# First attention layer of a fused two-block kernel: index projections first, selection dealt out in rounds, attention in head pairs, output projection in two halves

## The chip, the cores and the metric

The kernel runs on one core of a Trainium2 chip. The metric is device time in microseconds (us) of one execution. A core has TensorE (matrix products into PSUM), VectorE, ScalarE, GpSimd (POOL in the rows) and SyncE (SP, which issues DMAs). Each engine works through its own list of instructions in order, and the engines meet only at semaphores, which the kernel raises and waits for by hand.

## The reference, cut to what matters

Two blocks run one after the other on 512 tokens of width 1024. The second block prepends 16 meta tokens (528 positions) and has two attention layers. The change is in the first of these, a sparse attention that picks 128 keys for each query:

```python
q, k, v, qi, ki, wi = jnp.split(h @ w_in, A_SPLITS, axis=-1)      # 1024, 256, 256, 512, 64, 8 columns
q = rms_norm(q.reshape(B, Tp, N_HEADS, A_HEAD_DIM), gq)           # 8 heads of 128
k = rms_norm(k.reshape(B, Tp, A_KV_HEADS, A_HEAD_DIM), gk)        # 2 key/value heads
# for each block of queries
s = jnp.einsum('bqhd,bsd->bqhs', qib, ki) * IDX_DIM ** -0.5       # 8 index heads of 64
score = jnp.einsum('bqh,bqhs->bqs', wib, jax.nn.relu(s))
score = jnp.where(vis[None], score, NEG_INF)
_, idx = lax.top_k(score, k_top)                                  # 128 keys
# bias by relative position, softmax over the chosen keys, values
logits = jnp.einsum('bqgrd,bqkgd->bqgrk', qg, ksel) * scale + bias
o = jnp.einsum('bqgrk,bqkgd->bqgrd', softmax(logits), vsel)
out = o.reshape(...) @ w_o ;  h = h + out
```

## The kernel before, in words

**Numbers and weights.** Activations lie transposed, features on partitions and 528 positions along the row. A projection is computed to fp32 accuracy from two parts: weight and activation are each split into `hi` and `lo`, and TensorE does hi x hi, hi x lo and lo x hi. One output tile of 128 features takes 8 x 3 x 2 = 48 matmuls of 264 columns (L480). Its weights come by a DMA of 512 KB on SP's queue into `w_raw`, ScalarE makes `w_hi` (L405), VectorE makes `w_lo` (L411). Two slots of each let the splits of tile g+2 follow the products of tile g. The small fp32 matmuls (index scores, logits, transposes, values) are two records each in the profile.

**Queries in blocks.** The 528 queries are one block of 16 (i = 0) and four of 128 (i = 1 to 4). Block i sees 16, 144, 272, 400 or 528 keys. The selection finds the 128 largest scores of each query row by 16 rounds of MAX8 (the eight largest) and MATCH_REPLACE8 (strike them out), L2121 and L2122. From what was struck out comes a mask (`selm`, L2127), which GpSimd adds to the bias of each head (`msb`, L1030).

**The old order of this layer.** First all 17 tiles of `w_in_a` (`pa`, `kw`): q, k, v, index queries, and one with the index key and the head weights. ScalarE evacuates (L1245), GpSimd multiplies by the norm's inverse root (L612), and between tiles the ten q and k tiles are normalised by head: square, sum by TensorE (L1645), root, an inverse over 128x528 (L2089), product (L2090). Then 40 combinations (block i, head h), i outermost, in `combosA`. For each: logits on TensorE (L746, L748), bias and row maximum on VectorE (L2136), exponential on ScalarE (L1297), inverse and scaling on VectorE (L2153, L2154), transposes (L755, L757), their copies (L1310, L1313), the values' product (L766) and its copy (L1319). Logits of a combination, values of the one two before and transposes of the one before follow each other on TensorE. Ahead of the first head of a block i > 0 stand its eight index scores, the weighted sum of their relu on VectorE (L2111, L2115), the 16 rounds and the mask. At the end o is split, and the output projection `oa` has 8 tiles of 48 matmuls, which VectorE adds to the residual.

The second attention layer (another kind, `qkv` in the code) is already written with its projection tiles between the steps of the attention and with two heads to a step. The change doesn't touch its order; its lines (L1729 tiles, L1765 logits, L1784 and L1787 transposes, L1801 and L1803 values, L1385 exponentials, L2251 and L2254 row maxima, L1744 sums of squares by head) serve as a comparison.

## Time and profile before

| what | us |
|---|---|
| median of 3 runs | 2784.76 (2784.76 to 2785.87) |
| profiled execution, its own time | 2784.07 |
| its span | 2782.0 |
| TensorE busy | 2511.2 (90%) |
| VectorE busy | 1427.3 (51%) |
| ScalarE busy | 1038.6 (37%) |
| GpSimd busy | 489.1 (18%) |
| granted TensorE clock, mean | 0.922 |

The page divides the span into 40 slices of 69.6 us. In slices 20 to 23 (counted from 1), 1321 to 1600 us, where this attention layer lies, TensorE's digits are 6, 7, 5 and 7 against 8 and 9 nearly everywhere else, and those of the granted clock 6, 5, 5 and 8. A clock of 1.00 means 2.4 GHz and 0.50 means 1.2 GHz. How to read it: a stage in which TensorE has no gaps is bound by TensorE. Where it has gaps, the view of waits says which engine it waited for, and the chain of waits in order of time shows the pieces in which TensorE had no part.

### The profile page before, as it was taken

How to read it: one execution, taken by the hardware profiler on the slowest of the kernel's cores; microseconds unless marked ns; L12 is line 12 of the kernel's file. 1: busy time of each engine (PE TensorE's matmuls, PEld its weight loads, DVE VectorE, ACT ScalarE, POOL GpSimd, SP SyncE). 2: the span in 40 equal slices, each digit the busy share in tenths (PEclk: the TensorE clock that was granted, in tenths of full speed). 3: DMA queues.
4: the chain of work that ended last, by engine and by line, in shares of the span. 5: the costliest groups of instructions: out<-in, count | busy, mean ns of one | idle time of the engine just before them, and what ended most of it. 6: DMA issues, size and time to landing. Idle time of an engine off the chain costs nothing.

```text
span 2782.0 us, 41428 instructions
## 1 busy us (share of the span) xinstructions
PE 2511.2 (90%) x15393; PEld 2206.8 (79%) x15393; DVE 1427.3 (51%) x2067; ACT 1038.6 (37%) x1792; POOL 489.1 (18%) x427
## 2 busy tenths in 40 slices
PE   5898888999879999969675799999989989999998
PEld 4677766788658878859543699999988867999998
DVE  6895455522444324255756556664334344666631
ACT  5543444432523223223332333332245543333322
POOL 0000224431360000352101121110000000211100
PEclk8998999999989989979655899999999977999999
DMA  7561111332322333323100023333332210333322
GB/s 262 166 181 31 38 32 41 90 96 81 93 69 85 96 110 95 98 77 84 37 1 0 16 84 90 90 90 91 91 111 62 70 47 27 87 90 90 89 88 89
DMA packets 386952, 227.17 MB, mean 82 GB/s; under 512 B 10562, under 2 KB 377893, under 8 KB 386853
## 3 DMA queue, kind: packets, MB, share of 16 engines
q1 hardware_dynamic: 378085, 191.14, 24.3%
q0 software_dynamic: 8160, 32.53, 3.2%
q10 hardware_dynamic: 608, 2.16, 0.2%
q8 instruction: 65, 1.06, 0.2%
q14 instruction: 34, 0.28, 0.0%
HBM read 220.82 MB, written 4.85 MB: 81 GB/s over the span
## 4 chain that ended last, share of the span: by engine, by line
PE 76%; DVE 9%; issue 7%; ACT 3%; DMA 2%; POOL 2%; SPq 0%; POOLq 0%; ACTq 0%; DVEq 0%
PE PS L480 60%; PE PS L1729 5%; DMA w_raw<-in_w_in_dram 1%; DVE ada_acc L626 1%; PE PS L766 1%; PE PS L1586 1%; PE PS L1765 1%; PE PS L1801 1%; ACT w_hi L405 1%; DVE w_lo L411 1%; PE PS L1803 1%; PE PS L1598 1%; DVE conv_acc L1929 1%; DMA w_ada<-in_w_ada_dram 1%; POOL square L707 1%
## 5 line engine op out<-in xcount | busy, mean ns | idle before, releaser
L411 DVE TENSOR_TENSOR w_lo<-w_raw,w_hi 128x1024 fp32r<-128x1024 f32 x360 | 482.8, 1341 | 759.4 <-ACT w_hi L405 759.1
L480 PE MATMUL PS<-op_hi,w_hi 128*128 128x264 f32 (+3 forms) x2536 | 696.4, 329 | 45.3 <-DVE op_lo L582 16.2
L480 PE MATMUL PS<-op_lo,w_hi 128*128 128x264 f32 (+3 forms) x2536 | 690.1, 326 | 0.0
L480 PE MATMUL PS<-op_hi,w_lo 128*128 128x264 f32 (+3 forms) x2536 | 687.1, 325 | 0.0
L480 PEld LDWEIGHTS PS<-op_hi,w_hi 128*128 128x128 f32 (+2 forms) x2536 | 428.0, 190 | 102.8 <-issue 23.0
L405 ACT ACTIVATE w_hi<-w_raw 128x1024 fp32r<-128x1024 f32 x360 | 379.0, 1053 | 221.5 <-PE PS L480 200.3
L480 PEld LDWEIGHTS PS<-op_hi,w_lo 128*128 128x128 f32 (+2 forms) x2536 | 426.7, 191 | 38.3 <-issue 0.7
L480 PEld LDWEIGHTS PS<-op_lo,w_hi 128*128 128x128 f32 (+2 forms) x2536 | 427.1, 191 | 36.7 <-issue 0.9
L480 PE MATMUL PS<-ff_hi,w_hi 128*128 128x264 f32 (+1 forms) x960 | 242.2, 312 | 0.0
L480 PE MATMUL PS<-ff_hi,w_lo 128*128 128x264 f32 (+1 forms) x960 | 242.2, 312 | 0.0
L480 PE MATMUL PS<-ff_lo,w_hi 128*128 128x264 f32 (+1 forms) x960 | 242.1, 312 | 0.0
L1336 ACT ACTIVATE ff_u<-PS 128x528 f32<-128x528 f32 x88 | 53.9, 613 | 336.8 <-PE PS L480 317.3
L612 POOL TENSOR_TENSOR ff_u<-ff_u,rstd 128x528 f32<-128x528 f32 x88 | 100.3, 1141 | 421.7 <-ACT ff_u L1336 392.7
L480 PEld LDWEIGHTS PS<-ff_lo,w_hi 128*128 128x128 f32 x960 | 157.0, 188 | 9.9
L480 PEld LDWEIGHTS PS<-ff_hi,w_hi 128*128 128x128 f32 x960 | 156.9, 188 | 9.9
L480 PEld LDWEIGHTS PS<-ff_hi,w_lo 128*128 128x128 f32 x960 | 156.7, 188 | 10.0
L766 PE MATMUL PS<-probsT,v_tokA 128*128 128x128 f32 (+2 forms) x240 | 60.1, 387 | 76.1 <-ACT probsT L1313 75.6
L766 PEld LDWEIGHTS PS<-probsT,v_tokA 128*128 128x128 f32 (+1 forms) x240 | 45.2, 257 | 103.1 <-ACT probsT L1313 93.7
L679 POOL TENSOR_TENSOR sumsq<-sumsq,evac 128x528 f32<-128x528 f32 x21 | 28.0, 1332 | 515.9 <-ACT evac L662 515.9
L2065 DVE TENSOR_TENSOR norm_v<-evac 128x512 f32<-128x512 f32 x32 | 22.2, 692 | 107.2 <-ACT evac L1224 107.2
L2192 DVE SCALAR_TENSOR_TENSOR ff_c<-ff_u,param_cols,ff_c 128x528 f32<-128x528 f32 x88 | 69.8, 793 | 12.6 <-DVE ff_c L2191 6.7
L2191 DVE SCALAR_TENSOR_TENSOR ff_c<-ff_u,param_cols,ff_c 128x528 f32<-128x528 f32 x88 | 67.7, 769 | 12.6 <-DVE ff_c L2189 6.7
(403 smaller groups left out, 3743.5 us busy)
## 6 DMA issues: line engine op xcount, KB each, us to landing
w_raw<-in_w_up_dram SPq DMA_DIRECT2D x120, 512.0 KB, 3.8
w_raw<-in_w_in_dram SPq DMA_DIRECT2D x64, 512.0 KB, 4.1
w_raw<-in_w_down_dram SPq DMA_DIRECT2D x64, 512.0 KB, 3.7
w_ada<-in_w_ada_dram POOLq DMA_DIRECT2D x12, 2048.0 KB, 10.2
...
```

Of the source, the lines that this page charges most:

```text
L405: act.activation(whi[slot][:], wraw[slot][:], ACT.Copy).then_inc(sem("w_hi_ready"), 1)
L411: dve.tensor_tensor(wlo[slot][:], wraw[slot][:], whi[slot][:].bitcast(F32), ALU.subtract).then_inc(sem("w_split"), 1)
L480: last = pe.matmul(a[0:l.cols, h, 0:cn], w[slot][:, k, 0:l.cols], x[:, kk, c0:c0 + cn], start=(j == 0 and k == 0 and w is whi and x is l.h ...
L612: pool.tensor_tensor(x, x, rs[0:L[name].cols, :], ALU.mult).then_inc(sem("scaled"), 1)
L626: ins = dve.scalar_tensor_tensor(acc[:], w[:, k, :], small[:, 8 + k:9 + k], acc[:], ALU.mult, ALU.add)
L679: pool.tensor_tensor(sacc[:, :], sacc[:, :], et[g % 2][:, :], ALU.add).then_inc(sem("sumsq_ready"), 1)
L707: squared = link.mark(pool.tensor_tensor(sqt[:, c0:T], e, e, ALU.mult))
L766: last = pe.matmul(PS[:, b, 0:nq], v(t)[0:rows, :], p[0:rows, t, 0:nq], start=(t == 0), stop=(t == ntile - 1))
L1336: act.activation(halves(uu[par][:, 2:2 + T]), acc_view(l, par), ACT.Copy).then_inc(sem("evacuated"), 1)
L1729: last = pe.matmul(PS[:, h, 0:TH], w[slot][:, k, :], x[:, k, h * TH:(h + 1) * TH], start=(k == 0 and w is whi and x is hi), stop=(k == KD ...
L2191: link(dve.scalar_tensor_tensor(c[:, :], u[:, 1:1 + T], w(1), c[:, :], ALU.mult, ALU.add))
L2192: dve.scalar_tensor_tensor(c[:, :], u[:, 0:T], w(0), c[:, :], ALU.mult, ALU.add).then_inc(sem("ff_conv"), 1)
```

## The change

1. **Order of the tiles** (`TILES_A`): the four index-query tiles, the tile with index key and head weights, then k0, q0 to q3, v0, k1, q4, q5, v1, q6, q7. The first five run alone. The other twelve stand in slots 0 to 11 of a list of 22 slots, one tile each.
2. **Selection.** Index scores and their sums of block s+1 stand in slot s (0 to 3). The 64 rounds are dealt out over slots 0 to 12 (`ROUNDS`, rounds before and after the index sum). There are four relu buffers for two, and scores and masks of all four blocks have places of their own.
3. **Steps.** 16 steps (`STEPS_A`), each a pair of heads d and a batch b of query blocks (b = 0 is blocks 0 and 1, then one block each), run from slot 5 to 20. A slot has the logits of step n, a tile, the values of step n-1 and the transposes of step n. The values' product is now laid out by queries, so the division by the row sum is done in its copy (`outA`), and o is turned back by transposes (`turn_headA`) in slots 15, 16, 20, 21 and after.
4. **Norms.** Nothing is multiplied by the norm's inverse root over whole tiles. q and k are normalised from sums of squares by head, gathered by small matmuls in a 32x132 tile, in four batches (slots 3, 5, 9, 12). That tile takes a root and an inverse, goes to DRAM and comes back spread over all partitions (`head_rows_A`, on SP's queue). v takes its factor in its copy.
5. **Output projection.** `oa1` with o of heads 0 to 3, 8 half tiles of 24 matmuls, five in slots 17 to 21 and three after; `oa2` with heads 4 to 7, 8 half tiles. Both are added to the residual.

The core of the diff:

```diff
+        TILES_A = ("i0", "i1", "i2", "i3", "kw", "k0", "q0", "q1", "q2", "q3", "v0", "k1", "q4", "q5", "v1", "q6", "q7")
-        L["pa"] = Linear(plan, 16, wsrc(I["w_in_a_2"][0], 0), HH, HL, block1=False)
-        L["kw"] = Linear(plan, 1, wsrc(I["w_in_a_2"][0], 2048), HH, HL, cols=72, block1=False)
-        L["oa"] = Linear(plan, KD, wsrc(I["w_o_a_2"][0], 0), OAh, OAl, block1=False)
+        L["ia"] = Linear(plan, 17, lambda g, t, par, j, kt, cols: ia_src(g), HH, HL, block1=False)
+        for half in range(2):
+            L[f"oa{half + 1}"] = Linear(plan, KD, down_src(I["w_o_a_2"][0], 4 * half), *((HH, HL), (OAh, OAl))[half],
+                                        kts=(4,), block1=False)
+        SLOTS_A = 22
+        STEPS_A = [(0, 0), (0, 1), (1, 0), (1, 1), (0, 2), (1, 2), (2, 0), (2, 1), (0, 3), (1, 3), (3, 0), (2, 2), (3, 1),
+                   (2, 3), (3, 2), (3, 3)]
+        NORM_SLOT = {3: 0, 5: 1, 9: 2, 12: 3}
+        ROUNDS = {0: (0, 5), 1: (10, 0), 2: (6, 0), 3: (4, 0), 4: (3, 0), 5: (5, 0), 6: (5, 0), 7: (5, 0), 8: (5, 0),
+                  9: (4, 0), 10: (3, 0), 11: (5, 0), 12: (4, 0)}
+        FIRST_PART = 17
...
             # SyncE
+            def head_rows_A(b):
+                sp.wait_ge(sem("hn_rec"), b + 1)
+                sp.dma_start(head_scratch[b], head_msA[:]).then_inc(sem("hn_rows"), 16)
+                sp.wait_ge(sem("hn_rows"), 16 * (b + 1))
+                for n, (_, sq) in enumerate(NORM_TILES[b]):
+                    src = bass.AP(head_scratch.tensor, b * 32 * 132 + n * 132, [[0, P], [8 * 132, 4], [1, 132]])
+                    sp.dma_start(sq[:, :].rearrange("p (q n) -> p q n", q=4), src).then_inc(sem("hn_bc"), 16)
...
             # TensorE
+            def logitsA(n):
+                d, b = STEPS_A[n]
...
+                if n:
+                    pe.wait_ge(sem("A_max"), n)
+                    pe.wait_ge(sem("A_pt"), 2 * n)
...
+            for s in range(SLOTS_A):
+                n = step_at(s)
+                if s in NORM_SLOT:
+                    head_squaresA(s)
+                if s in (6, 10):
+                    turn_valuesA(s)
+                if s in (15, 16, 20, 21):
+                    turn_headA({15: 0, 16: 2, 20: 4, 21: 5}[s])
+                if n is not None:
+                    logitsA(n)
+                if s < 12:
+                    projectA(5 + s)
+                if s >= FIRST_PART:
+                    partA(s - FIRST_PART)
...
+                if s < 4:
+                    index_scores(s + 1)
...
+                if 0 <= s - 6 < len(STEPS_A):
+                    headsA(s - 6, s)
+                if n is not None:
+                    turn_probsA(n)
+                if s in (15, 16):
+                    turn_headA({15: 1, 16: 3}[s])
...
             # ScalarE
+                if n is not None:
+                    expA(n)
+                if s < 12:
+                    project_outA(5 + s)
...
+                if s < 4:
+                    index_relu(s + 1)
+                if 0 <= s - 6 < len(STEPS_A):
+                    outA(s - 6)
+                if n is not None:
+                    probs_outA(n)
...
             # VectorE
+                if n is not None:
...
+                    row_maxesA(n)
+                if norm is not None:
+                    dve.wait_ge(sem("hn_std"), norm + 1)
+                    dve.reciprocal(head_msA[:], head_msA[:]).then_inc(sem("hn_rec"), 1)
+                if s:
+                    select(ROUNDS.get(s, (0, 0))[0])
+                if s - 1 in NORM_SLOT:
+                    head_scaleA(NORM_SLOT[s - 1])
+                if s < 12:
+                    split_nextA(L["ia"], 5 + s)
+                if s < 4:
...
+                    index_sum(s + 1)
+                    select(ROUNDS[s][1])
+                if n is not None:
+                    sums_inverse(n)
```

VectorE before, at the end of the selection for query block 1; the lines are those of the code before (L2121 and L2122 one round, L2127 the mask, L2136 bias and row maximum of head 0, whose number behind a name is a buffer):

```order
L2121 MAX top_142<-idx_work 128x8
L2122 MATCH_REPLACE idx_work<-top_142,idx_work 128x144
L2127 TENSOR_SCALAR sel_mask<-idx_work 128x144
L2136 ISA probs_136,maxes<-PS,bias_sel_130 128x144
L2136 ISA maxes 128x1
L2143 TENSOR_SCALAR maxes<-maxes 128x1
L2153 RECIPROCAL maxes<-maxes 128x1
```

VectorE now, from the end of slot 7 into slot 8 (lines of the changed code: L422 weight split, L2387 inverse of the row sums, L2370 row maxima of two heads at 272 keys, L2347 and L2348 a round at 400 keys):

```order
L422 TENSOR_TENSOR w_lo_57<-w_raw_53,w_hi_55 128x1024
L2387 RECIPROCAL statsA<-statsA 128x4
L2370 ISA probsA_145,statsA<-PS,bias_sel_136 128x272
L2370 ISA statsA 128x1
L2370 ISA probsA_146,statsA<-PS,bias_sel_137 128x272
L2370 ISA statsA 128x1
L2378 TENSOR_SCALAR statsA<-statsA 128x2
L2347 MAX statsA<-idx_work 128x8
L2348 MATCH_REPLACE idx_work<-statsA,idx_work 128x400
```

Rounds of one block now stand behind the row maxima of steps with fewer keys, with a weight split between them.

TensorE before, in query block 4 (L757 and L755 transposes of one head, L748 the logits of the next, L766 the values of the one before):

```order
L757 MATMUL PS<-mats,probs_136 128x128 x4
L748 MATMUL PS<-projA 128x264 x2
L766 MATMUL PS<-probsT_141,v_tokA 128x128 x5
L755 MATMUL PS<-mats,probs_134 16x128
L757 MATMUL PS<-mats,probs_134 128x128 x4
```

TensorE now, from the end of the tile of slot 7 (L1752) into slot 8: values of a step (L1867, L1869), transposes of the next (L1847, L1850), then the logits of slot 8 (L1831) and the first products of its tile:

```order
L1752 MATMUL PS<-op_hi,w_lo_57 128x264 x2
L1867 MATMUL PS<-v_tokA,probsTA_147 128x128 x2
L1869 MATMUL PS<-v_tokA,probsTA_147 128x128
L1867 MATMUL PS<-v_tokA,probsTA_148 128x128 x2
L1869 MATMUL PS<-v_tokA,probsTA_148 128x128
L1850 MATMUL PS<-mats,probsA_143 16x16
L1847 MATMUL PS<-mats,probsA_143 128x128
L1850 MATMUL PS<-mats,probsA_143 16x128
L1850 MATMUL PS<-mats,probsA_144 16x16
L1847 MATMUL PS<-mats,probsA_144 128x128
L1850 MATMUL PS<-mats,probsA_144 16x128
L1831 MATMUL PS<-qk_A 128x272 x2
```

A projection tile of 48 matmuls stands between the logits of a step and its transposes.

ScalarE before, in query block 1 (L1297 the exponential of a head, L1319 the output of an earlier one, L1310 and L1313 copies of the transposed probabilities):

```order
L1297 ACTIVATE probs_135,maxes<-probs_135,maxes 128x144
L1319 ACTIVATE projA<-PS 128x128
L1310 ACTIVATE probsT_141<-PS 128x128
L1313 ACTIVATE probsT_141<-PS 16x128
```

ScalarE now, in slot 8 (L1346 exponentials, L1319 and L1320 copy and square of the tile, L416 weight split, L1357 the output copies of the step before, L1368 the copies of the transposed probabilities, L1397 the root for the head norms):

```order
L1346 ACTIVATE probsA_145,statsA<-probsA_145,statsA 128x272
L1346 ACTIVATE probsA_146,statsA<-probsA_146,statsA 128x272
L1319 ACTIVATE qk_A<-PS 128x528
L1320 ACTIVATE norm_v_71<-PS 128x528
L416 ACTIVATE w_hi_54<-w_raw_52 128x1024
L1357 ACTIVATE o_tokA<-PS,statsA 16x128
L1357 ACTIVATE o_tokA<-PS,statsA 128x128
L1357 ACTIVATE o_tokA<-PS,statsA 16x128
L1357 ACTIVATE o_tokA<-PS,statsA 128x128
L1368 ACTIVATE probsTA_147<-PS 128x384
L1368 ACTIVATE probsTA_148<-PS 128x384
L1397 ACT_TABLE_LOAD
```

The copies of the transposed probabilities, which the logits of the next step wait for, stand behind the evacuation and split of the tile.

## Rows read from the trace of the kernel before

**Rows 1.** Busy time by stretch: length, engines busy (instructions), PEclk, DMA share, GB/s.
```profile
1238.40:1349.00 110.60, 108.42 (x830) 106.03 (x828) 68.85 (x40) 38.32 (x55) 28.25 (x23) 0.98 0.34 94
...
1384.00:1395.00 11.00, 10.87 (x38) 7.97 (x38) 4.20 (x23) 5.37 (x23) 1.94 (x4) 0.50 0.01 2
...
1502.00:1542.00 40.00, 18.27 (x73) 12.35 (x71) 32.04 (x65) 7.50 (x18) 0.86 (x1) 0.59 0.00 0
```

**Rows 2.** Chain of waits in order of time: start us, us, what.
```profile
1239.12 8.72 PE PS L480 x54
...
1279.89 5.85 PE PS L480 x48
...
1349.13 30.96 issue
...
1574.37 60.23 PE PS L480 x480
...
2245.35 3.73 PE PS L1744 x32
```

**Rows 3.** Waits, 1238 to 1640 us: total us, times, longest.
```profile
POOL bias_sel L1030 <- DVE sel_mask L2127: 142.1, 4, 40.9
```

**Rows 4.** Timeline of VectorE, selection of blocks 1 and 4.
```profile
1368.55 0.31 DVE L2121 MAX8 top<-idx_work 128x8 f32<-128x144 f32 x1
...
1369.30 0.31 DVE L2121 MAX8 top<-idx_work 128x8 f32<-128x144 f32 x1
...
1515.83 0.71 DVE L2121 MAX8 top<-idx_score 128x8 f32<-128x528 f32 x1
...
1517.38 0.71 DVE L2121 MAX8 top<-idx_work 128x8 f32<-128x528 f32 x1
```

**Rows 5.** Groups by line and form, 1238 to 1640 us: busy us, mean ns.
```profile
L2115 DVE SCALAR_TENSOR_TENSOR idx_score<-relu,wi_tok,idx_score 128x528 f32<-128x528 f32 x7 | 5.4, 768 | 2.8 <-ACT relu L1288 2.6
...
L2115 DVE SCALAR_TENSOR_TENSOR idx_score<-relu,wi_tok,idx_score 128x144 f32<-128x144 f32 x7 | 2.6, 369 | 1.6 <-ACT relu L1288 1.2
```

**Rows 6.** Instructions on w_raw, whole span: min/median/max ns.
```profile
L411 DVE TENSOR_TENSOR w_lo<-w_raw,w_hi x360: 1208/1227/2130, 55.5 to 2761.7; 128x1024 fp32r<-128x1024 f32 x180
```

**Rows 7.** Timeline of ScalarE in the second attention layer.
```profile
2143.59 0.61 ACT L1374 ACTIVATE projB<-PS 128x528 f32<-128x528 f32 x1 [3.31 <-PE PS L1729]
...
2144.59 1.06 ACT L405 ACTIVATE w_hi<-w_raw 128x1024 fp32r<-128x1024 f32 x1
```

**Rows 8.** Groups by line and form in the second layer, 2060 to 2260 us.
```profile
L1385 ACT ACTIVATE probsB<-probsB,statsB 128x528 f32<-128x528 f32 x12 | 8.7, 729 | 9.9 <-DVE statsB L2259 9.9
...
L2254 DVE CUSTOM_DVE_ANT_0 probsB<-PS,bias 128x528 f32<-128x528 f32 x12 | 8.0, 705 | 30.3 <-PE PS L1765 30.3
...
L1396 ACT ACTIVATE probsTB<-PS 128x512 f32<-128x512 f32 x10 | 5.6, 589 | 0.3 <-PE PS L1787 0.3
```

**Rows 9.** Busy time by stretch, second layer with its tiles, and without.
```profile
2070.00:2252.00 182.00, 174.65 (x1278) 152.56 (x1277) 72.06 (x226) 100.26 (x307) 0.00 (x0) 0.96 0.21 56
2270.00:2330.00 60.00, 48.39 (x196) 32.92 (x194) 28.85 (x97) 31.98 (x114) 0.00 (x0) 0.56 0.06 18
```

**Rows 10.** Chain of waits, heads of query block 4, 1545 to 1575 us.
```profile
1548.41 1.76 PE PS L748 x4
...
1552.39 0.89 PE PS L748 x4
1553.28 1.51 PE PS L766 x10
```

**Rows 11.** Chain of waits, head factors of the second layer through DRAM.
```profile
2252.10 1.40 DMA head_scratch<-head_ms
...
2259.07 7.41 DMA w_raw<-in_w_o_b_dram
```

**Rows 12.** Timeline of ScalarE at a change of function table.
```profile
2247.31 1.28 ACT L1445 ACT_TABLE_LOAD   x1
2249.42 0.31 ACT L1445 ACTIVATE head_ms<-head_ms 32x132 f32<-32x132 f32 x1 [0.82 <-DVE head_ms L2317]
```

More of the change, by code:

```diff
@@ L266, in two_block_program @@
+        SCR = (None, 0, 144, 416, 816)
         pbt = at("projB", [P, 8, T], F32, F + 16896)
@@ L569, in two_block_program @@
         SCALED, _done = {}, 0
-        for _l in ("pa", "kw", "f0u", "f1u"):
+        for _l in ("f0u", "f1u"):
             SCALED[_l] = _done
@@ new lines, in two_block_program, with qk_tile, step_at, expsA @@
+        assert sum(sum(r) for r in ROUNDS.values()) == 64
+        FIRST_PART = 17
+        def qk_tile(name):
+            return qk[:, int(name[1]) + (8 if name[0] == "k" else 0), :]
+        def step_at(s):
+            return s - 5 if 0 <= s - 5 < len(STEPS_A) else None
+        def expsA(n):
+            return sum(4 if b == 0 else 2 for _, b in STEPS_A[:n + 1])
+        def last_step(h):
+            return STEPS_A.index((h // 2, 3))
+        def lgA_parts(b, i, hp):
+            _, nq, nk, _ = TT[i]
+            if b < 3:
+                c = 144 if i == 0 else 0
+                return [(PS[0:nq, 4 + hp, c:c + nk], 0, nk)]
+            return [(PS[0:nq, 2 + hp + 2 * a, 0:nk // 2], a * nk // 2, nk // 2) for a in range(2)]
@@ new lines, in partA @@
+            def partA(f):
+                l = L["oa1"]
+                slot = (l.U0 + f) % 2
+                pe.wait_ge(sem("evacuated"), l.G0 + f + 2)
+                pe.wait_ge(sem("w_split"), l.U0 + f + 3)
+                if f == 0:
+                    pe.wait_ge(sem("oA_ready"), 4)
+                for k in range(4):
+                    for w, x in ((whi, HH), (whi, HL), (wlo, HH)):
+                        for h in range(2):
+                            last = pe.matmul(PS[:, h, 0:TH], w[slot][:, k, :], x[:, k, h * TH:(h + 1) * TH],
+                                             start=(k == 0 and w is whi and x is HH),
+                                             stop=(k == 3 and w is wlo))
+                last.then_inc(sem("units_done"), 1)
@@ new lines, in head_squaresA @@
+            def head_squaresA(s):
+                b = NORM_SLOT[s]
+                tiles = NORM_TILES[b]
+                dst = PS[0:32, 6 if b else 3, 0:132]
+                pe.wait_ge(sem("evacuated"), L["ia"].G0 + max(TILES_A.index(name) for name, _ in tiles) + 3)
+                if b:
+                    pe.wait_ge(sem("idx_relu"), 32)
+                if s > 6:
+                    pe.wait_ge(sem("A_o"), 2 * (s - 6))
+                for q4 in range(4):
+                    for n, (_, sq) in enumerate(tiles):
+                        r = 8 * q4 + n
+                        last = pe.matmul(dst, sel_one[:, 31 - r:63 - r], sq[:, 132 * q4:132 * q4 + 132],
+                                         start=(q4 == 0 and n == 0), stop=(q4 == 3 and n == len(tiles) - 1))
+                last.then_inc(sem("hn_sum"), 1)
@@ L2173, in feed_forward @@
+            part_add(5)
+            head_loA(6)
+            part_add(6)
+            head_loA(7)
+            part_add(7)
+            l = L["oa2"]
+            for g in range(KD):
+                r = halves(R[:, g, :])
+                dve.wait_ge(sem("units_done"), l.U0 + g + 1)
+                dve.tensor_tensor(r, r, acc_view(l, g % 2), ALU.add).then_inc(sem("evacuated"), 1)
+                split_nextA(l, g)
+                gained_lo(dve, "n4", ffn_gain(0), HH, HL, g)
             def feed_forward(x, name):
```

784 lines of the change are left out of this document (467 added, 317 removed).

## The prediction

> **What bounds the kernel now.** I read the busy table by stretch first. From 1238.4 to 1349 us TensorE projects the 17 tiles, busy 108.4 of 110.6 us at a granted clock of 0.98. From 1349 to 1574 comes the attention, 225 us. In the last of its four selection stretches TensorE is busy 18.3 us of 40 at a clock of 0.59, and even a stretch in which it is busy all the time, 1384 to 1395, has 0.50, that is 1.2 GHz [rows 1]. The chain in order of time says the same: one projection tile of 48 matmuls takes 5.85 us, then pieces of 30 us and more stand there with no work of TensorE ("issue"), and from 1574.37 the output projection runs back to back [rows 2]. The waits name the cause: GpSimd waits 142.1 us in four pieces for the selection mask [rows 3]. Those are the index sums and the 16 rounds of MAX8 and MATCH_REPLACE8 on VectorE, which no other work accompanies. So this layer is bound by TensorE, then by VectorE four times over, then by the hand-over of one head at a time.
>
> The stretch that the change rebuilds starts with tile 1 at 1239.12 and ends with the last of 384 output matmuls. The last chain piece has 480 in 60.23 us, so 384 take 48.2, the end is 1622.6, and the stretch is 383.5 us [rows 2]. Outside it nothing changes but semaphore names.
>
> **The change part by part, from the start of tile 1.**
>
> (a) Tiles 1 to 4. Tile 1 costs 8.72 as before (it starts at the lower clock), three more 5.87 each. The sums for the norm between them are larger: four 264-column records as now (0.9), eight of the 132-column kind at 3.73/32 = 0.12, ten tiny ones, 2.8 in all [rows 2]. Sum 29.1 us.
>
> (b) Slots 0 to 4. The order of VectorE shows what they hold. A round has a period of 0.75 us at 144 keys and 1.55 at 528 [rows 4], so by the line between them 1.02 at 272 and 1.28 at 400. Slots 0 to 4 have 16 rounds at 144 and 12 at 272: 24.2 us. The four index sums have 8 instructions each of 0.37 to 0.77 us [rows 5]: 3.0, 4.0, 5.1 and 6.1, 18.2 together. Five weight splits at 1.23 [rows 6] are 6.1, three scalings of q and k, of the score update's kind and size, at 0.77 are 2.3, root and inverse of the head sums 2.7, small ones 0.6. VectorE's load is 54.1. It begins 8.5 after (a): one tile, the evacuation and the split on ScalarE, which in the second attention layer take 2.06 together (2143.59 to 2145.65) [rows 7]. VectorE is not always fed. The weight split waits for a tile that TensorE can start only when the index scores before it have gone, four relu buffers ahead at most, and in that wait TensorE's clock should fall for a tile or two. I put 8 us for this (bounds 0, a perfect interleave, and 20, a full tile of waiting in three slots). 8.5 + 54.1 + 8 = 70.6.
>
> (c) Slots 5 to 11. VectorE has 5 to 8 us of rounds, 1.23 of split, 1.2 of row maxima and up to 2.3 of scaling: 9.2 to 10.5 a slot. TensorE has a tile of 6.05 and 3 to 4 us of small matmuls. Longest is a loop through ScalarE. Logits of a step, then the tile, then evacuation, square and split (2.06), then the output copies of the previous step (0.45 to 0.8), then the copies of the transposed probabilities (0.59 each at 512 columns) [rows 8], and only then may the next logits start, because both read the count of those copies. The order of ScalarE shows this row by row. For slots 6 to 11: tiles 36.3, evacuation and split 12.0, logits 5.8, outputs 3.4, probability copies 5.2, hand-overs 2.4, the head sums in slot 9 that no other work covers 2.0: 67.1, or 11.2 a slot. Slot 5 costs 9.1, since nothing of a previous step hangs on it. Together 76.2. The second layer, built from the same pieces, holds clock 0.96 over 182 us [rows 9], so I take the full clock here.
>
> (d) Slots 12 to 16 have no tile. The step is a bare loop: logits, row maxima (0.71 a head at 528), exponentials (0.73 a head) [rows 8], transposes, copies. The end of the second layer is the like stretch: 60 us at clock 0.56, TensorE busy 48 [rows 9]. At the lower clock the logits of one head at 528 keys cost 1.76, at the full one 0.89 [rows 10]. For a step with 528 keys at 1.2 GHz: logits 3.5, values of the step before 5.3, transposes 2.1, copy and hand-over 1.1, 12.0. Slots 12 to 16 come to 10.5, 12, 12, 11 and 13, where slot 16 holds three of the chained turns of o (turn, split high, split low). Sum 58.5; at the full clock it would be 44 (values of a head at 528 keys are 1.51 then [rows 10]). I take the lower clock, because that is what the like stretch had.
>
> (e) Slots 17 to 21 put half a tile (24 matmuls, 2.94) into each step: 8.9, 9.3, 9.3, 10.6 and 6.5, 44.6 at the full clock. At 1.2 GHz everywhere it would be 66. I take 54.6, nearer to the full clock than (d), since the dense half tiles fill the gaps. (f) Three half tiles and two turns at the end, each waiting for its one accumulator: 14. (g) The second half of the output projection, 8 x 2.94 = 23.5, with an estimated 2 us a tile of VectorE and of ScalarE beneath it.
>
> What hides without cost: the 64 rounds' other 36 on (c) and in slot 12; the scaling of v moved into its copy; four round trips through DRAM for the head factors, which in the second layer took 7.0 us from the first issue to the weight load behind them (2252.10 to 2259.07) [rows 11], with most of a slot's rounds ahead of the scaling that needs them; the loads of w_in_a, 512 KB each, which wait in SP's queue behind those trips (if that cover fails, one tile starts up to 4 us late). GpSimd's 17 scalings fall away, its mask adds double up in one step of two heads.
>
> Sum: 29.1 + 70.6 + 76.2 + 58.5 + 54.6 + 14 + 23.5 = 326.5, against 383.5: 57.0 less. The profiled execution took 2784.07 (span 2782.0), 0.7 under the median shown, so the forecast is 2784.76 - 57 = 2728 us.
>
> One price depends on a view. Exp and Sqrt need different tables; the order of ScalarE has five loads in the attention, two of them in slot 12, where nothing covers them. The trace shows 1.28 us for a load, at 2247.31, and a Sqrt that started at 2249.42, 0.83 after the load's end, released by VectorE and not by the load [rows 12]. I take 1.28. The Trainium skill ("ScalarE: Activation LUTs", What ACT_TABLE_LOAD costs) adds a drain of about 1.38 us to each. By that rule slot 12 would be 2.8 longer and the time 2731; by the trace the gap behind the load is too short for the whole drain.
>
> **The rivals.**
> *The clock stays at 2.4 GHz.* Then (d) falls by 14.5, (e) by 10 and the waits in (b) by about 5: 87 less, 2698. For it: once the heads with 528 keys run back to back in the old attention, the logits drop from 1.76 to 0.89 [rows 10]. Against: the like stretch at 0.56.
> *VectorE sets the pace.* If index sums and rounds are stretched by GpSimd's adds beside them (the split w_lo has a median of 1227 ns and a maximum of 2130 [rows 6]) and each slot's hand-overs add to VectorE's load and don't hide beneath it, slots 0 to 4 cost 10 more and slots 5 to 11 cost 13 each, 91 for 76: 25 more, 2753. For it: VectorE's load of 10 is within 1 us of the loop's 11. Against: its work in a slot is needed only a slot later.
> *Slower: the tiles lose their clock.* In the old attention TensorE was busy 10.87 of 11 us and still had 0.50 [rows 1]. If small fp32 matmuls between the tiles hold the clock there, each of 12 tiles costs 4.7 more (56), the half tiles outside my allowance 19, logits and sums of slots 5 to 11 another 8: with 4 already in (b) that is 79, and the time is 2784.8 - 57 + 79 = 2807. It turns slower once all 12 tiles run low. Against: the second layer's 0.96 with the same mixture [rows 9].
> *The rounds don't get hidden.* If selection of one query block still held up the next step, the 36 rounds of (c) and slot 12, about 50 us, would come back and leave some 7 of gain, 2778. Against: the order puts each round behind row maxima already released, and a mask is asked for only slots later.
>
> **How the numbers follow.** Forecast 0.55, own range 2710 to 2745. Clock stays up 0.18, VectorE's pace 0.18, rounds not hidden 0.04, slower 0.05. The range 2697 to 2757 takes in the first three and the bounds of (b), (d) and (e). 0.2% is 5.6 us, about what can be told from no change. Faster 0.93, same 0.02 (the edge of the fourth case), slower 0.05.
>
> **What would show it.** In the changed profile the wait for the selection mask falls from 142 us to under 15; the stretch from tile 1 to the last half tile is about 327 us; slots 6 to 11 are 11 us apart, and the wait ahead of their logits ends with the copies of transposed probabilities; TensorE's clock is above 0.95 there and about 0.5 to 0.6 in slots 12 to 16. I am wrong if slots 6 to 11 are longer than 12.5 with VectorE busy throughout, if tiles take 10 us and more, or if any time outside the stretch moves by more than 3 us.

## The result and the profile after

| | before | changed |
|---|---|---|
| median, us | 2784.76 (2778.16 to 2785.87, 4 runs) | 2701.76 (2700.22 to 2705.56, 4 runs) |
| ratio | | 0.9716 (95% interval 0.970 to 0.9732) |
| profiled execution, its span | 2784.07, 2782.0 | 2700.63, 2698.8 |
| mean granted clock | 0.922 | 0.949 |

The change is 83 us, not the 57 of the forecast. The time lies near the lower edge of the whole range (2697 to 2757) and outside the forecast's own (2710 to 2745): it is in the part that belonged to the rival "the clock stays at 2.4 GHz" (2698).

First the windows by stretch of the changed kernel, with the columns of [rows 1]: slots 8, 12 to 16, 13 alone, 17 to 21, and the tail of three half tiles.

```profile
1376.10:1389.20 13.10, 12.96 (x95) 11.24 (x95) 9.19 (x25) 6.18 (x14) 4.46 (x4) 1.00 0.22 61
...
1423.90:1466.00 42.10, 32.21 (x169) 23.89 (x169) 19.57 (x57) 19.69 (x60) 13.03 (x12) 0.85 0.08 16
...
1428.90:1442.00 13.10, 6.37 (x31) 5.02 (x31) 8.77 (x17) 3.54 (x10) 6.90 (x6) 0.80 0.23 43
...
1466.00:1508.20 42.20, 40.29 (x274) 34.74 (x273) 15.29 (x40) 18.66 (x48) 4.69 (x4) 0.98 0.09 26
1508.20:1520.20 12.00, 11.11 (x84) 10.08 (x83) 5.12 (x10) 3.60 (x8) 0.00 (x0) 1.00 0.22 66
```

Where [rows 1] had 18.3 us of work in 40 at clock 0.59, slots 17 to 21 are at 0.98. Even slots 12 to 16, with the one large gap in them (slot 13), have 0.85, not the 0.56 of [rows 9] on which the forecast was built. Slot 8 ends with 2.9 us of head sums.

The chain of waits in order of time (start, us, what) answers to [rows 2]:

```profile
1245.07 8.57 PE PS L1752 x54
...
1256.66 17.73 PE PS L1752 x144
...
1278.13 4.75 DMA ki_twice<-ki_wi
...
1364.43 1.17 PE PS L1831 x8
...
1373.81 0.94 ACT w_hi L416
...
1375.25 0.74 ACT probsTA L1368 x2
...
1376.13 1.16 PE PS L1831 x4
...
1520.16 35.52 PE PS L491 x288
```

Slot 0 starts at 1256.66 + 17.73 = 1274.39. Of the last piece 192 matmuls are `oa2`: 35.52 x 192/288 = 23.7, so the stretch ends at 1543.8 and is 298.8 us long, against 383.5. The pieces from 1364.43 to 1376.13 are slot 7: logits, tile, evacuation, weight split, output copies, probability copies, next logits. That is the loop through ScalarE that the forecast named.

The wait for the mask did not go away, though. This row of the view of waits (us, times, longest) answers to [rows 3]:

```profile
POOL bias_sel L1081 <- DVE sel_mask L2350: 127.7, 4, 43.2
```

GpSimd still stands idle for 127.7 us, only because it has nothing else to do. Only the end of the last of the four waits reaches TensorE. Its timeline (start, us, line, what, idle time before it and what ended it) shows where:

```profile
1432.35 0.48 PE L1869 MATMUL PS<-v_tokA,probsTA 16*128 16x128 f32 x2
1438.63 1.11 PE L1847 MATMUL PS<-mats,probsA 128*128 128x128 f32 x4 [5.80 <-ACT probsA L1346]
...
1493.20 2.02 PE L1831 MATMUL PS<-qk_A 128*128 128x264 f32 x8
```

In slot 13 TensorE waits 5.8 us: the last four rounds stand in slot 12, behind them mask, GpSimd's add, row maxima, exponential. The last row, slot 20, shows logits of two heads at 528 keys in 2.02 us, the level of 0.89 a head in [rows 10], not of 1.76.

### The profile page after: what moved, and what is told of

Its sections match the earlier page's. It is cut to its first block, busy times and chain, and to the rows that moved or that the text cites. A ratio compares the mean times of both kernels' runs of the same rounds, so it can differ in the third digit from the quotient of the medians.

```text
span 2698.8 us, 41478 instructions
## 1 busy us (share of the span) xinstructions
PE 2491.0 (92%) x15491; PEld 2198.9 (81%) x15491; DVE 1375.8 (51%) x2004; ACT 1041.7 (39%) x1782; POOL 469.8 (17%) x415
## 3 DMA queue, kind: packets, MB, share of 16 engines
q1 hardware_dynamic: 383685, 193.91, 25.6%
## 4 chain that ended last, share of the span: by engine, by line
PE 78%; DVE 10%; issue 4%; ACT 4%; DMA 3%; POOL 2%; SPq 0%; POOLq 0%; ACTq 0%; DVEq 0%
PE PS L491 58%; PE PS L1963 5%; PE PS L1752 3%; DVE ada_acc L637 1%; DMA w_raw<-in_w_in_dram 1%; PE PS L1687 1%; PE PS L1999 1%; PE PS L2035 1%; ACT w_hi L416 1%; PE PS L1767 1%; PE PS L1831 1%; DVE w_lo L422 1%; PE PS L2037 1%; PE PS L1699 1%; DVE conv_acc L2163 1%
## 5 line engine op out<-in xcount | busy, mean ns | idle before, releaser
L422 DVE TENSOR_TENSOR w_lo<-w_raw,w_hi 128x1024 fp32r<-128x1024 f32 (+1 forms) x368 | 476.4, 1295 | 750.7 <-ACT w_hi L416 749.9
L491 PE MATMUL PS<-op_hi,w_hi 128*128 128x264 f32 (+2 forms) x2264 | 633.3, 330 | 30.9 <-DVE op_lo L569 10.9
L491 PE MATMUL PS<-op_lo,w_hi 128*128 128x264 f32 (+2 forms) x2264 | 630.4, 329 | 0.0
L491 PE MATMUL PS<-op_hi,w_lo 128*128 128x264 f32 (+2 forms) x2264 | 627.4, 328 | 0.0
L416 ACT ACTIVATE w_hi<-w_raw 128x1024 fp32r<-128x1024 f32 (+1 forms) x368 | 380.8, 1035 | 243.8 <-PE PS L491 210.6
L491 PEld LDWEIGHTS PS<-op_hi,w_hi 128*128 128x128 f32 (+1 forms) x2264 | 382.0, 189 | 82.3 <-issue 12.9
L491 PEld LDWEIGHTS PS<-op_hi,w_lo 128*128 128x128 f32 (+1 forms) x2264 | 381.1, 189 | 38.5 <-issue 1.0
L491 PEld LDWEIGHTS PS<-op_lo,w_hi 128*128 128x128 f32 (+1 forms) x2264 | 381.2, 189 | 37.5 <-issue 1.4
L1752 PE MATMUL PS<-op_hi,w_hi 128*128 128x264 f32 (+1 forms) x272 | 62.6, 314 | 16.3 <-DVE op_lo L593 16.2
L2488 DVE SCALAR_TENSOR_TENSOR ff_c<-ff_u,param_cols,ff_c 128x528 f32<-128x528 f32 x88 | 70.4, 800 | 12.6 <-DVE ff_c L2487 6.7
L714 POOL TENSOR_TENSOR resid<-resid,evac 128x512 f32 (+1 forms) x16 | 20.9, 1305 | 302.5 <-ACT evac L655 302.5
```

The costliest lines, as they stand in the source:

```text
L416: act.activation(whi[slot][:, 0:ks, :], wraw[slot][:, 0:ks, :], ACT.Copy).then_inc(sem("w_hi_ready"), 1)
L422: dve.tensor_tensor(wlo[slot][:, 0:ks, :], wraw[slot][:, 0:ks, :], whi[slot][:, 0:ks, :].bitcast(F32), ALU.subtract).then_inc(sem("w_split ...
L491: last = pe.matmul(a[0:l.cols, h, 0:cn], w[slot][:, k, 0:l.cols], x[:, kk, c0:c0 + cn], start=(j == 0 and k == 0 and w is whi and x is l.h ...
L1752: last = pe.matmul(PS[0:rows, b + h, 0:TH], w[slot][:, k, 0:rows], x[:, k, h * TH:(h + 1) * TH], start=(k == 0 and w is whi and x is HH), ...
L2488: dve.scalar_tensor_tensor(c[:, :], u[:, 0:T], w(0), c[:, :], ALU.mult, ALU.add).then_inc(sem("ff_conv"), 1)
```

## The experiments

Every kernel below is an edit of the changed kernel. The table gives the median, its ratio with the interval (to the kernel before, timed again beside each group of runs), and four distances read from TensorE's timeline as starts of the logits. Slots 0 to 4 are taken from the end of tile 1 (so with tiles 2 to 4) to the logits of slot 5. "17 to 19" runs from the logits of slot 17 to those of slot 20.

| kernel | median | ratio (95%) | 0 to 4 | 6 to 11 | 12 to 16 | 17 to 19 |
|---|---|---|---|---|---|---|
| changed | 2701.76 | 0.9716 (0.970, 0.9732) | 91.1 | 70.4 | 42.2 | 27.2 |
| changed, again | 2702.31 | 0.9709 (0.969, 0.9729) | 99.0 | 70.3 | 42.2 | 27.2 |
| rounds undealt | 2742.18 | 0.9849 (0.9824, 0.9875) | 139.1 | 70.4 | 35.9 | 27.2 |
| rounds late | 2721.17 | 0.977 (0.9743, 0.9798) | 98.0 | 70.1 | 64.7 | 27.3 |
| half tiles late | 2714.53 | 0.976 (0.9734, 0.9787) | 94.7 | 68.8 | 40.8 | 18.4 |
| waits before exponentials | 2717.57 | 0.976 (0.9735, 0.9786) | 99.0 | 70.3 | 55.3 | 27.8 |
| both of these | 2746.01 | 0.9872 (0.984, 0.9904) | 94.5 | 70.4 | 55.1 | 29.4 |
| extra work on VectorE | 2719.06 | 0.9771 (0.9756, 0.9786) | 102.4 | 77.1 | 42.2 | 27.2 |
| extra work on ScalarE | 2707.47 | 0.973 (0.9705, 0.9755) | 99.0 | 76.1 | 42.1 | 27.2 |
| two relu buffers | 2707.52 | 0.9723 (0.9708, 0.9738) | 98.3 | 70.5 | 42.1 | 27.2 |
| rounds early | 2699.05 | 0.9686 (0.9669, 0.9703) | 94.6 | 72.1 | 34.2 | 26.9 |
| rounds early, refined | 2691.43 | 0.968 (0.9658, 0.9702) | 92.9 | 68.9 | 34.4 | 26.8 |
| the same, split moved | 2695.68 | 0.9682 (0.9662, 0.9702) | 97.9 | 70.0 | 35.4 | 27.3 |

**The changed kernel again.** No edit.

> The changed kernel itself again, as the base for kernels that differ from it by few us: 2701.8, within 0.2%.

It came out at 2702.31. Its profile shows how much two executions of one program differ inside. Windows of 10 us in slots 0 to 4, first of the changed kernel, then of its repetition:

```profile
1290.00:1300.00 10.00, 7.39 (x51) 5.96 (x49) 9.11 (x41) 3.31 (x7) 0.00 (x0) 1.00 0.00 0
...
1310.00:1320.00 10.00, 7.94 (x43) 4.96 (x42) 7.66 (x16) 5.54 (x11) 0.00 (x0) 1.00 0.20 52
...
1330.00:1340.00 10.00, 9.60 (x63) 8.11 (x64) 9.00 (x19) 3.69 (x7) 0.00 (x0) 1.00 0.27 73
```

```profile
1290.00:1300.00 10.00, 7.39 (x22) 5.03 (x23) 8.79 (x27) 3.96 (x10) 0.00 (x0) 0.58 0.20 52
...
1310.00:1320.00 10.00, 10.00 (x37) 6.27 (x37) 4.29 (x9) 2.52 (x5) 0.00 (x0) 0.56 0.20 52
...
1330.00:1340.00 10.00, 10.00 (x37) 7.73 (x36) 6.95 (x14) 3.40 (x6) 0.00 (x0) 0.54 0.21 54
```

Tiles of slots 1 to 4 run at one clock or the other from execution to execution, 8 us in all. The start of the stretch differs as well. The whole shift is there before the stretch begins, at the end of the products of the projection ahead of it (chain from 1180 us on; 1208.70 in the changed kernel, 1203.17 in its repetition), and both have the same seven pairs of residual add and split on VectorE behind that:

```profile
1179.90 28.80 PE PS L491 x127
```

```profile
1179.81 23.36 PE PS L491 x103
...
1239.53 8.71 PE PS L1752 x54
```

Tile 1 starts at 1239.53 here, at 1245.07 in the profile above, at 1239.12 in [rows 2]. Slot 7 is not the same everywhere either. First the changed kernel, then "half tiles late", which has no edit in this slot:

```profile
1364.40:1376.10 11.70, 11.12 (x74) 10.10 (x75) 8.07 (x25) 4.66 (x15) 0.00 (x0) 0.85 0.17 46
```

```profile
1362.30:1372.40 10.10, 9.52 (x75) 8.50 (x75) 8.03 (x26) 4.66 (x15) 0.00 (x0) 1.00 0.20 54
```

So a single profile says nothing of edits under some 8 us unless their own slots are compared, and in slots 6 to 11 nothing of 1.5 us unless slot 7 had the same clock. Why one execution has the lower clock in these places and another does not stays open.

**Rounds undealt.**

```diff
-        ROUNDS = {0: (0, 5), 1: (10, 0), 2: (6, 0), 3: (4, 0), 4: (3, 0), 5: (5, 0), ...
+        ROUNDS = {0: (0, 16), 1: (0, 16), 2: (0, 16), 3: (0, 16)}
```

> The changed kernel with the 16 rounds of each query block done at once behind its index sum (slots 0 to 3), nothing dealt out. The changed kernel is at 2701.8. Theory (dealing hides the rounds, slots 5 to 11 are paced by the loop through ScalarE): slots 0 to 3 take the rounds' whole 73.6 us instead of 21.1, slot 4 loses 3.1 and the gap of 5.8 before slot 13 goes, so +43: 2745 (2735 to 2755), and slots 6 to 11 stay 11.0 to 11.8 apart. Rival (VectorE sets the pace of slots 5 to 11 now): they shrink by about 2 us each once the rounds are gone: 2731. Second rival (the rounds are not what the change gained by): 2710 or less.

40.4 us more than the changed kernel. Slots 6 to 11 keep their 70.4 us to a tenth, though VectorE lost all its rounds there: the first theory, and VectorE does not set the pace. Dealing out is worth about half of the 83 us. All engines in slots 0 to 4 (columns as above), VectorE busy 99.4 of 118 us:

```profile
1274.00:1392.00 118.00, 65.52 (x366) 52.68 (x364) 99.38 (x244) 24.93 (x51) 5.69 (x6) 0.72 0.13 32
```

**Rounds late.** All 16 rounds of block 4 in slot 12.

```diff
-                  9: (4, 0), 10: (3, 0), 11: (5, 0), 12: (4, 0)}
+                  12: (16, 0)}
```

> The changed kernel with all 16 rounds of query block 4 in slot 12, so that TensorE's gap before the transposes of slot 13 grows from 5.8 us by twelve rounds of 1.55, to some 24 us. Theory A (the clock follows the work around it; slots 13 to 21 are dense enough to bring it back): +18.6 and a little, 2721 (2717 to 2725), logits of slots 15 and later at the full clock. Theory B (a long gap sets the clock low, and steps without tiles keep it there, as in the end of the second layer): slots 14 to 16 take the 1.2 GHz values and slots 17 to 21 part of them, +19 +14 +10 to 20: 2745 to 2755.

2721.17, theory A. Windows of TensorE alone (length, busy, clock, DMA share, GB/s) in the gap and behind it:

```profile
1450.00:1460.00 10.00, 0.00 (x0) 0.50 0.00 0
...
1470.00:1480.00 10.00, 9.73 (x59) 0.82 0.01 2
...
1490.00:1500.00 10.00, 10.00 (x47) 0.63 0.00 0
1500.00:1510.00 10.00, 9.27 (x65) 1.00 0.09 28
```

TensorE stands idle for 22.7 us, until 1464.11. For the next 33 us the clock is low most of the time, with a full stretch in between, though TensorE is hardly idle: 10.00 of 10.00 us busy at 0.63 in one window. Slots 14 to 16 take 28.0 us for 24.0 in the changed kernel. From slot 17 on the clock is full: the low clock is not handed on.

**Half tiles late.**

```diff
-        FIRST_PART = 17
+        FIRST_PART = 22
...
-            partA(5)
+            for f in range(6):
+                partA(f)
```

> The changed kernel with all eight half tiles of the first output projection behind slot 21 and none in slots 17 to 21. Theory A (the half tiles lie mostly in TensorE's waits; the clock does not need them): slots 17 to 21 become 7 to 7.5 us for 9, 5 x 1.7 less, and 5 x 2.94 = 14.7 come back behind them: +6, 2708 (2703 to 2712), clock 1.00 in slots 17 to 21. Theory B (only the dense half tiles hold the clock there): those slots run at 1.2 GHz, 11 to 12 us each, +22 more: 2730.

```profile
1460.00:1485.00 25.00, 21.70 (x130) 17.10 (x131) 7.45 (x28) 13.23 (x39) 4.86 (x5) 1.00 0.00 1
```

The clock is 1.00 in slots 17 to 20 with no dense work in them: theory A on what it was to decide. Slots 17 to 19 shrink by 8.8 us, where 8.5 was expected of all five slots from 17 to 21. The stretch behind them grew by 19.6 us and not by the 14.7 expected: from the logits of slot 20 to the end of the last half tile 45.8 us for 26.2. So from slot 17 on it is 10.8 us more, and the median 12.8, not 6. What made the half tiles behind the slots dearer than expected was not taken apart.

**Waits before the exponentials.**

```diff
+                if 7 <= n <= 15:
+                    for r in range(4):
+                        if (n, r) > (7, 0):
+                            act.wait_ge(sem("dum"), 4 * (n - 7) + r)
+                        act.activation(dumA[:], HH[:, 7, :].bitcast(F32), ACT.Copy).then_inc(sem("dum"), 1)
                 for i in BATCH[b]:
```

> The changed kernel with four extra chained 128x528 copies on ScalarE ahead of the exponentials of slots 12 to 20, about 3 us a step, so that TensorE's busy share in these steps falls from 0.9 to about 0.7. Theory A (a step only gets longer by its wait, TensorE keeps 2.4 GHz): +20 to 27, 2725. Theory B (at that share the clock falls to 0.5 to 0.6 as at the end of the second layer): logits of two heads at 528 keys take 3.5 and not 2.0, steps are 4 to 5 us longer beyond the copies: 2745 or more.

```profile
1428.00:1483.00 55.00, 38.47 (x170) 26.67 (x168) 18.90 (x57) 32.30 (x81) 12.99 (x12) 0.74 0.07 15
1483.00:1525.00 42.00, 39.39 (x266) 34.14 (x265) 14.11 (x40) 27.03 (x64) 4.70 (x4) 0.98 0.09 26
```

Both theories were wrong in part. In the slots without tiles the clock did fall (0.74), and they became 13.1 us longer, close to the copies' own 5 x 2.67 = 13.4. It looks as if the slower TensorE cost nothing, but two things cancel. The changed kernel has its 5.8 us wait for the mask in slot 13, and here the copies lie over it: the row maxima of slot 13 wait for the logits and no longer for the mask (VectorE):

```profile
1440.69 0.71 DVE L2379 CUSTOM_DVE_ANT_0 probsA<-PS,bias_sel 128x528 f32<-128x528 f32 x1 [2.85 <-PE PS L1837]
```

The kernel to compare with is "rounds early" below, which has no such wait either. Slots 13 to 16, here and there:

```profile
1437.70:1483.70 46.00, 33.72 (x146) 24.08 (x147) 10.43 (x37) 25.04 (x64) 12.99 (x12) 0.72 0.01 1
```

```profile
1434.10:1463.30 29.20, 25.31 (x146) 18.38 (x147) 9.41 (x36) 15.14 (x49) 7.09 (x8) 0.94 0.10 20
```

That is 16.8 us more for 4 x 2.67 = 10.7 of copies. The other 6 us or so go with the lower clock: the logits of slot 14 take 3.86 us for 2.02. In the changed kernel slots 13 to 16 are 37.1 us, 7.9 of them the wait for the mask and the low clock behind it; that the copies took away, and slot 12 grew by 4.3, by the copies and a table load of 1.28 that now stands behind them. In slots 17 to 19 the same copies cost 0.6 us: the half tile lies over them.

**Both edits at once.** `FIRST_PART = 22` and the copies, as in the two diffs above.

> Both earlier edits at once: no half tile in slots 17 to 21, and four chained copies (2.67 us as measured) ahead of the exponentials of slots 12 to 20. It asks whether the steps of this layer fall to 1.2 GHz as those at the end of the second layer did, once no dense work stands between them and TensorE is busy for 0.6 to 0.7 of each. With half tiles late alone the profile had steps of 5.0, 7.1 and 6.2 us there at clock 1.00. Theory A (the clock stays): each becomes 2.7 longer, slots 17 to 20 at clock 0.9 or more, 2714.5 + 13 (what the copies cost slots 12 to 16) + 11 = 2738. Theory B (what a step holds beside its waits decides the clock; at 0.6 to 0.7 it falls): slots 17 to 20 at 0.5 to 0.6, logits of two heads at 528 keys 3.6 to 3.9 us for 2.0, 10 to 12 us a step, 2745 to 2750.

Slots 17 to 20 of this kernel, and below them slots of the second attention layer in the changed kernel:

```profile
1482.00:1521.00 39.00, 27.56 (x129) 21.21 (x129) 7.61 (x28) 22.68 (x54) 4.62 (x4) 0.81 0.00 1
```

```profile
2180.00:2230.00 50.00, 37.08 (x151) 23.81 (x151) 27.67 (x88) 26.45 (x96) 0.00 (x0) 0.58 0.14 40
```

The median, 2746, fits theory B, the clock fits neither (0.81, with the logits of two heads at 3.12 us in slot 18 and 2.02 in slot 20). Three slots are 11.0 us longer than without the copies, 8.0 of it the copies. So waits in the steps do bring the clock down by themselves. The second layer's 0.58 at a like busy share (37.1 of 50 us, for 27.6 of 39 here) is not reproduced.

**Extra work on VectorE.** An inverse over 128x528 (3.45 us) in slots 1 to 10.

```diff
+                if 1 <= s <= 10:
+                    dve.reciprocal(dumA[:], R[:, 7, :])
```

> The changed kernel with one extra inverse over 128x528 (3.44 us) on VectorE in each of the slots 1 to 10. Slots 1 to 4 have no slack: +13.8 in every theory. Theory A (the loop through ScalarE paces slots 5 to 10, VectorE only fills its idle 1.0, 0.5, 3.6, 3.9, 1.6 and 3.1 us): +7.5 more, 2723 (2717 to 2726). Theory B (VectorE sets the pace): each costs its whole 3.44 there too, 34.4 in all: 2736.

Slots 6 to 11, where the six inverses of slots 5 to 10 show, took 6.7 us more (7.5 expected; 20.6 if VectorE had set the pace): theory A. Slots 1 to 4 were to cost 13.8 in every theory and cost 3.4 against the repetition, whose clock from tile 2 to slot 4 is the same (0.80, and 0.79 here; 0.92 in the first profile). VectorE had some 10 us of slack there in executions in which TensorE ran low; no run added to VectorE in one at the full clock.

**Extra work on ScalarE.**

```diff
+                if 6 <= s <= 11:
+                    for r in range(2):
+                        if (s, r) > (6, 0):
+                            act.wait_ge(sem("dum"), 2 * (s - 6) + r)
+                        act.activation(dumA[:], HH[:, 7, :].bitcast(F32), ACT.Copy).then_inc(sem("dum"), 1)
```

> The changed kernel with two extra chained 128x528 copies (1.3 us together) on ScalarE behind the weight split of slots 6 to 11, ahead of the output copies. Theory A (the prediction's: the copies of the transposed probabilities, behind evacuation, square and split, pace these slots): 6 x 1.3 = 8 more, 2710, slots 6 to 11 12.3 and more apart. Theory B (TensorE's own work fills the slots and ScalarE has slack): under 2 more, and the slots stay 11.0 to 11.9 apart.

5.7 us more in slots 6 to 11, of the 7.8 that the copies take: theory A's side, short of its 8. It is 1.2, 1.9 and 1.2 in slots 6 to 8, where slot 7 has a little less clock too (0.81 for 0.85), and 0.3 to 0.7 in the others. The chain shows the copy in the loop, before the next logits:

```profile
1377.78 0.94 ACT w_hi L417
1378.72 0.54 ACT dumA L1411
...
1380.45 0.58 ACT probsTA L1369 x2
...
1381.16 1.16 PE PS L1837 x4
```

**Two relu buffers.**

```diff
-                    if m >= 4:
-                        act.wait_ge(sem("idx_sum"), m - 3)
+                    if m >= 2:
+                        act.wait_ge(sem("idx_sum"), m - 1)
...
-                        dve.tensor_scalar(scr_of(i), rl[m % 4][:, 0:nk], w, None, ALU.mult).then_inc(sem("idx_sum"), 1)
+                        dve.tensor_scalar(scr_of(i), rl[m % 2][:, 0:nk], w, None, ALU.mult).then_inc(sem("idx_sum"), 1)
...
```

> The changed kernel with two relu buffers for four. Theory A (the prediction's: the index scores are released early by the four buffers, and so TensorE starts the next tile before VectorE has done the sums): two more of eight sums stand ahead of each tile in slots 0 to 3, 0.8 to 1.5 us each, of which TensorE's slack covers a part: 2706 (2703 to 2710). Theory B (slots 0 to 4 are VectorE's alone): no difference, 2701.8 within 1.

The median is 5 us above the repetition's, the ratios' intervals overlap, and its slots 0 to 4 (98.3) lie between those of two executions of the changed kernel. Inconclusive.

**Rounds early, and refined.** First 6, 6, 6, 5, 5, 4, 4 rounds in slots 5 to 11; then 5, 5, 6, 6, 5, 4, 5, with the wait for the doubled key one score later.

> The changed kernel with six, six, six, five, five, four and four rounds in slots 5 to 11 and none in slot 12, so that the mask of query block 4 is there a slot earlier. Theory A (the gap before slot 13 is the last mask's, and slots 5 to 11 have room on VectorE): the idle 5.8 us goes and the next logits stay at the full clock (2.0 for 3.9): 7.7 less, 2694 (2692 to 2698). Theory B (VectorE has no room in slots 5 to 11): four rounds of 1.3 to 1.55 come back there as 4 to 6 us, and the time is 2699 to 2702.

The gap and the low clock behind it went, 8.0 us in slots 12 to 16, and 1.7 came back in slots 6 to 11: the logits of slot 7 wait 1.6 us for VectorE's scaling of q and k, which the sixth round delays, and slot 7 is 1.0 longer at a clock of 0.78 for 0.85. The median, 3.3 lower, can't be told from the repetition's alone.

```diff
-                  9: (4, 0), 10: (3, 0), 11: (5, 0), 12: (4, 0)}
+        ROUNDS = {0: (0, 5), 1: (10, 0), 2: (6, 0), 3: (4, 0), 4: (3, 0), 5: (5, 0), 6: (5, 0), 7: (6, 0), 8: (6, 0),
+                  9: (5, 0), 10: (4, 0), 11: (5, 0)}
...
+                    if m == 1:
+                        pe.wait_ge(sem("kid_in"), 16)
...
-                    pe.wait_ge(sem("kid_in"), 16)
```

> The changed kernel with five, five, six, six, five, four and five rounds in slots 5 to 11 and none in 12, and with the wait for the doubled index key moved from ahead of the first index score to ahead of the second, the first that reads it. Theory: the gap of 5.8 us before slot 13 and the low clock behind it go without the 1.7 us that six rounds each in slots 5 and 6 cost, and the 1.8 to 2.4 us that TensorE waits for the copy of the index key shrink to about 1.5: 8 to 9 less than the changed kernel, 2693 (2690 to 2697). Rival (such microseconds are lost in the differences between two executions of slots 0 to 4, which were 91 to 99 us in the profiles): within 3 of 2699, the time with the first redealing.

```profile
1423.90:1454.00 30.10, 25.55 (x147) 18.95 (x148) 9.41 (x36) 15.64 (x52) 7.17 (x9) 0.94 0.09 20
```

TensorE's wait for the doubled index key, in the changed kernel and here:

```profile
PE PS L1808 <- DMA ki_twice<-ki_wi: 2.4, 1, 2.4
```

```profile
PE PS L1810 <- DMA ki_twice<-ki_wi: 1.1, 1, 1.1
```

Slots 12 to 16 take 34.4 us for 42.2, and slots 6 to 11 pay nothing: their 68.9 for 70.4 is slot 7 at the full clock (10.2 for 11.7), as in "half tiles late". At 2691.43 this is the fastest kernel here: 3.2% under the kernel before. Its lead over the changed kernel is 10 us by the medians, 8 by the slots' distances; the intervals of the two ratios overlap by a little.

**The weight split moved.** An edit of the refined kernel. ScalarE's split of the next weights goes from behind the evacuation to behind the copies of the transposed probabilities:

```diff
-                split_hi(act, l, g // 2, g % 2, 0, split_ks(l, g))
+                if g < 11:
+                    split_hi(act, l, g // 2, g % 2, 0, split_ks(l, g))
...
                 if n is not None:
                     probs_outA(n)
+                if 6 <= s <= 11:
+                    split_hi(act, L["ia"], (5 + s) // 2, (5 + s) % 2, 0, split_ks(L["ia"], 5 + s))
```

> The kernel with the redealt rounds and the later wait for the index key (2691.4), and in slots 6 to 11 ScalarE's weight split (about 1 us) moved from behind the evacuation to behind the copies of the transposed probabilities, so that it stands no longer between a tile and the next logits. Theory A (the loop through ScalarE paces slots 6 to 8 and half of 9 to 11, as the two extra copies showed with 5.7 us for 7.8): up to what TensorE idles in these slots now, 0.2 to 0.8 us each, 2 to 4 less: 2688, slots 6 and 7 under 10.8 apart. Theory B (the later w_hi makes VectorE's w_lo and with it a tile late): nothing or 1 to 6 more, 2692 to 2697.

Nothing gained that can be told (2695.68, ratio 0.9682 for 0.968). Slots 6 to 11 take 70.0 us for 68.9, but slot 7 has the lower clock again (a tile of 6.61 us for 5.85, below). Against the changed kernel, whose slot 7 has it too, slots 6 and 7 are 10.8 and 11.5 us long for 11.0 and 11.7, slot 8 is 0.1 shorter and the others are the same to 0.1. Their chain:

```profile
1357.69 5.85 PE PS L1755 x48
1363.54 0.32 PE PS L1874 x2
...
1365.43 0.43 PE PS L1874 x2
...
1366.76 0.47 ACT probsTA L1369
1367.37 1.53 PE PS L1836 x8
1368.90 6.61 PE PS L1755 x48
1375.52 0.44 PE PS L1872 x4
```

The tile is now followed by TensorE's own values and transposes, and ScalarE has only the last copy in the chain. TensorE's own work with the last copy is only 0.1 to 0.2 us a slot shorter than the loop, so taking ScalarE's share out gives next to nothing, while adding to it costs.

## Why the prediction was right, and what was off

By its steps, with the profile of the changed kernel and of its repetition:

| step | forecast | changed | again |
|---|---|---|---|
| (a) tiles 1 to 4, sums | 29.1 | 29.3 | 29.5 |
| (b) slots 0 to 4 | 70.6 | 69.9 | 77.8 |
| (c) slots 5 to 11 | 76.2 | 79.5 | 79.3 |
| (d) slots 12 to 16 | 58.5 | 42.2 | 42.2 |
| (e), (f) slots 17 to 21, tail | 68.6 | 54.2 | 54.1 |
| (g) second half of the output | 23.5 | 23.7 | 23.7 |
| stretch | 326.5 | 298.8 | 306.6 |

**The direction and most of the size** were right for the stated reasons. The rounds are hidden: undone, they cost 40 us, and slots 6 to 11 don't notice them. The loop through ScalarE paces these slots, as adding to it showed, though in a near tie with TensorE's own work: TensorE waits 0.6 to 0.9 us for the copies ahead of the logits of slots 6, 7, 8 and 11, and not at all ahead of those of slot 9. The term was sized 3 us short: 1.5 of it is the lower clock in slot 7, 0.9 the head sums at the end of slot 8 (2.9 us for the 2.0 taken; TensorE is busy 12.96 of 13.10 there). (a) and (g) hold to 0.4 us.

**What failed is one choice in (d) and again in (e): "I take the lower clock, because that is what the like stretch had."** With the full-clock values that the prediction gave beside it, 44 and 44.6 us, the forecast would have been 2703. That this comes within 2 us of the result is in part luck: without the gap in slot 13, which was not foreseen, slots 12 to 16 take 34.2 to 34.4 us, 10 less than 44, and the gap with the low clock behind it puts 8 back. The end of the second layer was like in its list of operations, not in how full it keeps TensorE: its rows in the changed kernel have 37.1 us busy in 50 even at the low clock, at which the same logits take twice as long [rows 10]. The new steps are fuller: the refined kernel has TensorE busy 25.6 of 30.1 us at 0.94. The prediction's own terms did not settle it. At the full clock its step of 528 keys had two logits (1.8), two values (3.0) and the transposes (1.1) in about 9 us, which is emptier than the steps came out. The heads of 528 keys in [rows 10], busy without such gaps, had come back to the full clock; that row was listed for the rival and given 0.18, against a row from another layer. So the total fell inside the range because the range took in this rival, not because the forecast's own account of (d) and (e) held. The runs show both halves: without any dense work the steps of this layer keep 1.00 (half tiles late), and with 2.67 us of wait added to each they go to 0.74 to 0.81. What makes the second layer's clock lower still, at a like busy share, stays open.

**"About 0.5 to 0.6 in slots 12 to 16"** was thereby wrong: 0.85 over all, low in and behind the 5.8 us gap and for a moment at the end of slot 16. That gap the prediction did not foresee; it counted "the 64 rounds' other 36 on (c) and in slot 12" as free, but the mask of block 4 is asked for one slot after its last round.

**"The wait for the selection mask falls to under 15"** was wrong as a test. It is 127.7 us, on an engine that had nothing else to do. The right test was what TensorE waits for.

**(b)** came out right in one execution and 7 us short in the next, for TensorE's clock between the index scores, which its allowance of 8 us named. That VectorE's load bounds these slots is not shown. Even in the faster execution it is busy 51.1 of 69.9 us, less than TensorE:

```profile
1274.40:1344.30 69.90, 56.78 (x364) 47.47 (x364) 51.07 (x133) 24.79 (x51) 2.02 (x4) 0.90 0.21 53
```

With 13.8 us more on VectorE, in an execution at the lower clock, these slots took 3.4 more. The rival "VectorE sets the pace" is refuted for slots 5 to 11. Of the two rivals on the slow side, rounds not hidden did not occur; tiles did lose their clock in slots 1 to 4 of the repetition (0.54 to 0.58), but hardly behind these.

**The time outside the stretch** moved by 5.9 us ahead of it and by 4.4 the other way behind it, over the 3 us named. The repetition, the same program, has 0.4 and 0.5: these are differences between executions.

**The table loads in slot 12** answer the question left open. ScalarE's timeline:

```profile
1424.60 1.28 ACT L1346 ACT_TABLE_LOAD   x1
1425.90 0.52 ACT L1346 ACTIVATE probsA<-probsA,statsA 128x272 f32<-128x272 f32 x1
```

The exponential starts 0.02 us behind the end of the load, so the price is 1.28, as taken. The drain that the Trainium skill ("ScalarE: Activation LUTs", What ACT_TABLE_LOAD costs) adds is not seen behind this load.

Not settled: the 40 us of the gain that are not the dealt rounds come from steps by pairs with a tile between, the norms without GpSimd and the output projection in halves. No run took these apart.
